# Folding the pooling map into w_out, and channel statistics from pair sums, in an 8-core streaming encoder layer

## The chip, the cores and the metric

The kernel runs as one program on the 8 cores of a Trainium2 chip, in two dies of four cores. Each core has TensorE (PE; its weight loads are shown apart as PEld), VectorE (DVE), ScalarE (ACT), GpSimd (POOL) and SyncE (SP), and 16 DMA engines. Every core computes its own stream with its own copy of the weights in its memory; the cores exchange nothing. The time is device time of the slowest core, in microseconds.

## The reference

One trunk layer, in float32. `x` is 8192 frames of a new stream (positions from 0) and 16 frames of a running one, of width 1024:

```python
z = x @ w_in + b_in                      # 1024 -> 1536: u (512) | a (512) | g (512)
v = a * sigmoid(g)
# mixer A: trailing mean over w frames (w = 2, 4, 8, 16, one group of 128 channels each) minus u
d = stack([(end - start) / count - u_new for each group])
A = einsum('blgc,gcd->blgd', d, w_pool) * pool_scale       # 4 maps of 128 x 128
# mixer B: causal depthwise convolution of width 31, LayerNorm over 512 channels, silu
B = silu(layer_norm(conv(v) + conv_b, ln_g, ln_b))
h = layer_norm(alpha * x + concat(A, B) @ w_out + b_out)
y = layer_norm(alpha * h + square(relu(h @ w_up)) @ w_down) # 1024 -> 4096 -> 1024
```

The outputs are `y`, and the last 15 rows of u and 30 of v of each stream. Beside the layer norms nothing is non-linear between `d` and `w_out`, which is what lets the pooling map and its scale be multiplied into the upper 512 rows of `w_out`.

## The kernel before

**Tiles.** A core's frames are cut into tiles of 512, the last 512 into two of 256; the 16 frames of the running stream ride with the second last tile. That makes 17 tiles, m = 0 to 16. Channels lie on the partitions for the input projection, the pooling, the convolution and the feed-forward up; frames lie on them for `w_out`, the down projection and both big layer norms.

**Weights.** They are 21 blocks of 1024 x 512 in f32 in `wblk`: b = 0 to 2 `w_in`, 3 and 4 `w_out`, 5 to 12 `w_up`, 13 to 20 `w_down`. A block comes into one of the four slots of the ring `wring` either by a casting DMA from `wblk`, issued by POOL, or by a plain DMA from `wscr`, a bf16 copy in memory, issued by SP. `LATE` names, for some blocks, the tile in which the copy is first stored; until then the block is cast anew each time. Blocks in `DIRECT` are cast from memory to memory, `wblk` to `wscr`. The three other first blocks lie in `rb` in tile 0. `paced` lets a first-round cast wait until the one two or three places before it has landed; POOL issues and waits in order, and SP too.

**PE's program** (`pe_thread`). It is: `inproj` of tile 0, `inproj(0)` of tile 1, `stats` (the channel sums of tile 0: eight matmuls against a matrix of ones), `poolmap` (four matmuls), `wout` of tile 0, the rest of tile 1's `inproj` with tile 0's `transposes`. From then on a round has `up` and `down` of tile m-1, with `poolmap` and `stats` of tile m inside the second half of `down`, then `inproj(0)` of tile m+1, `wout` of tile m, and so on. The round is the steady state. In every engine the order is fixed when the program is built: `Sched.run` takes the operation that can start first by estimated durations, with a small window in which the lower `prio` wins.

**The work off PE.** POOL makes the windows: `window` writes `dbf`, from which `poolmap` and, on ACT, `poolout` (L857) make the first four chunks of `mix`. DVE makes the convolution, 31 taps for each of four chunks of channels (L763; L714 in tile 0), into `acc`. Tile 0 is special: its chunks 0, 2 and 3 are on DVE (`conv0_dve`), chunk 1 is scaled by ACT (L729) and added up by POOL (L734, `conv0_pool`). `prep` then has ACT write `acc` and its square as bf16 (L796, L797); `stats` adds them up, `lnconv` and `lnapply` (L823 to L842) normalise and write the last four chunks of `mix`. `wout` needs all eight. POOL adds `b_out` to the rows of x (`xload`, L864), and the layer norms' gain and shift rows (L910, L912, L1022, L1024).

**Constant rows.** Five rows of 1024 (`rows`) are read by a broadcasting DMA to all 128 partitions (`late_loads`, L395, on ACT's queue, once tile 0's u is out), and three are scaled by ACT (L402).

## Time and profile before

| | before |
|---|---|
| time of the two runs shown, us | 2548.84 and 2615.7, median 2582.27 |
| the profiled execution, us | 2545.76 |
| its span on the slowest core (core 0), us | 2544.7 |
| spans of the other cores, us | 2533.2 to 2544.0 |
| mean granted TensorE clock, of full speed | 0.982 to 0.985 |
| busy, share of the span: PE, DVE, ACT, POOL | 95%, 74%, 47%, 51% |
| chain that ended last: on PE, on DMA, on DVE | 90%, 4%, 3% |
| PE busy in the 40 slices of 64 us | 4, 2, 9, 8, then 9 or more throughout |
| HBM read and written, MB | 486.68 and 55.82 |

The span runs from the first to the last instruction; 1.06 us of the profiled time lie outside it. The two runs shown differ by 2.6%; the lower one is near the profiled execution.

PE is busy in nearly all of the span, except for the first 130 us or so, and a little up to 260 us. A busy digit for PE says that matmuls were in flight, not how much they did.

### The profile page before, as it was taken

How to read it: one execution, taken by the hardware profiler on the slowest of the kernel's cores; microseconds unless marked ns; L12 is line 12 of the kernel's file. 1: busy time of each engine (PE TensorE's matmuls, PEld its weight loads, DVE VectorE, ACT ScalarE, POOL GpSimd, SP SyncE). 2: the span in 40 equal slices, each digit the busy share in tenths (PEclk: the TensorE clock that was granted, in tenths of full speed). 3: DMA queues.
4: the chain of work that ended last, by engine and by line, in shares of the span. 5: the costliest groups of instructions: out<-in, count | busy, mean ns of one | idle time of the engine just before them, and what ended most of it. 6: DMA issues, size and time to landing. Idle time of an engine off the chain costs nothing.

```text
span 2544.7 us, 39217 instructions; the slowest of 8 cores (2533.2 to 2544.7 us)
## 1 busy us (share of the span) xinstructions
...
## 2 busy tenths in 40 slices
...
GB/s 172 133 137 207 234 199 216 224 199 161 189 211 176 198 180 202 159 186 179 182 199 182 199 158 185 188 182 195 181 203 146 185 188 181 189 200 178 228 250 234
DMA packets 79184, 483.17 MB, mean 190 GB/s; under 512 B 11808, under 2 KB 12064, under 8 KB 29760
## 3 DMA queue, kind: packets, MB, share of 16 engines
...
q14 instruction: 108, 0.88, 0.1%
HBM read 486.68 MB, written 55.82 MB: 213 GB/s over the span
## 4 chain that ended last, share of the span: by engine, by line
PE 90%; DMA 4%; DVE 3%; issue 2%; ACT 0%; another core or an unknown queue 0%; POOL 0%; DVEq 0%; ACTq 0%; POOLq 0%; SPq 0%
PE bank L486 88%; DMA sb_wring<-wblk 2%; DVE bank L714 1%; DMA sb_wring<-wscr 1%; PE bank L940 1%; DMA sb_rb<-wblk 1%; PE bank L809 1%; PE bank L806 0%; DVE sb_acc L839 0%; DVE sb_stat L1004 0%; DVE sb_xr L1002 0%; DVE sb_xr L1044 0%; DVE sb_xr L1047 0%; ACT sb_rb L899 0%
## 5 line engine op out<-in xcount | busy, mean ns | idle before, releaser
L763 DVE SCALAR_TENSOR_TENSOR bank<-sb_vext,sb_params,bank 128x512 f32<-128x512 f32 (+1 forms) x1856 | 1169.5, 714 | 0.1
L486 PE MATMUL bank<-sb_wring,sb_rb 128*128 128x512 bf16 x4092 | 904.8, 380 | 6.8 <-DMA sb_wring<-wscr 3.1
L486 PE MATMUL bank<-sb_hT,sb_wring 128*128 128x512 bf16 (+2 forms) x4231 | 883.7, 368 | 22.2 <-DMA sb_wring<-wblk 15.4
L486 PEld LDWEIGHTS bank<-sb_hT,sb_wring 128*128 128x128 bf16 x4320 | 423.4, 98 | 479.7 <-issue 27.1
L486 PEld LDWEIGHTS bank<-sb_wring,sb_rb 128*128 128x128 bf16 (+1 forms) x4160 | 405.8, 98 | 497.2 <-issue 11.6
L977 ACT ACTIVATE sb_rtmp<-bank 128x512 f32<-128x512 f32 (+2 forms) x544 | 308.7, 571 | 185.0 <-PE bank L486 180.9
L978 ACT ACTIVATE sb_rb<-sb_rtmp 128x512 bf16<-128x512 f32 (+2 forms) x544 | 323.4, 604 | 41.2 <-ACT sb_rtmp L977 2.6
L922 POOL TENSOR_TENSOR sb_stat<-sb_stat,sb_cst 128x1 f32<-128x1 f32 x128 | 71.2, 556 | 519.1 <-DVE sb_stat L920 518.8
L486 PE MATMUL bank<-sb_xT,sb_wring 128*128 128x512 bf16 (+2 forms) x1477 | 314.0, 366 | 1.4
L1002 DVE TENSOR_TENSOR sb_xr<-bank,sb_xr 128x512 f32<-128x512 f32 x130 | 89.5, 688 | 284.7 <-PE bank L486 284.7
L864 POOL TENSOR_TENSOR sb_xr<-sb_xr,sb_row 128x1024 f32<-128x1024 f32 (+1 forms) x65 | 152.4, 2370 | 246.2 <-DMA sb_xr<-xp 246.1
L857 ACT ACTIVATE sb_mix<-bank,sb_params 128x512 bf16<-128x512 f32 (+2 forms) x68 | 39.8, 662 | 419.5 <-PE bank L486 419.5
L486 PE MATMUL bank<-sb_wring,sb_mix 128*128 128x512 bf16 (+1 forms) x1021 | 228.7, 381 | 7.5 <-ACT sb_mix L857 6.1
L486 PEld LDWEIGHTS bank<-sb_xT,sb_wring 128*128 128x128 bf16 x1504 | 144.9, 98 | 148.7 <-issue 0.4
L899 ACT ACTIVATE sb_rb<-sb_xr,sb_stat 128x1024 bf16<-128x1024 f32 (+1 forms) x65 | 80.5, 1238 | 203.0 <-POOL sb_stat L924 189.4
L486 PEld LDWEIGHTS bank<-sb_wring,sb_mix 128*128 128x128 bf16 (+1 forms) x1040 | 101.5, 98 | 132.0 <-issue 12.5
L1022 POOL TENSOR_TENSOR sb_xr<-sb_xr,sb_row 128x1024 f32<-128x1024 f32 (+1 forms) x63 | 148.2, 2364 | 14.8 <-ACT sb_xr L1020 14.8
L910 POOL TENSOR_TENSOR sb_xr<-sb_xr,sb_row 128x1024 f32<-128x1024 f32 (+1 forms) x65 | 152.1, 2362 | 0.2
L912 POOL TENSOR_TENSOR sb_xr<-sb_xr,sb_row 128x1024 f32<-128x1024 f32 (+1 forms) x65 | 152.0, 2358 | 0.3
L1024 POOL TENSOR_TENSOR sb_xr<-sb_xr,sb_row 128x1024 f32<-128x1024 f32 (+1 forms) x63 | 148.1, 2362 | 0.3
L824 DVE SCALAR_TENSOR_TENSOR sb_lnq<-bank,sb_lnq 128x512 f32<-128x512 f32 (+2 forms) x17 | 11.2, 660 | 177.7 <-ACT sb_lnq L823 177.7
L645 POOL TENSOR_TENSOR sb_ptmp<-sb_uext 128x526 f32<-128x526 f32 (+1 forms) x68 | 68.2, 1013 | 91.3 <-ACT sb_uext L623 91.3
...
## 6 DMA issues: line engine op xcount, KB each, us to landing
sb_wring<-wscr SPq DMA_DIRECT2D x323, 1024.0 KB, 5.2
...
sb_wring<-wblk POOLq DMA_DIRECT2D x27, 1024.0 KB, 13.2
sb_xT<-xpt POOLq DMA_DIRECT2D x14, 1024.0 KB, 10.6
wscr<-sb_wring SPq DMA_DIRECT2D x12, 1024.0 KB, 8.9
wscr<-wblk POOLq DMA_DIRECT2D x6, 1024.0 KB, 27.1
wscr<-sb_rb SPq DMA_DIRECT2D x3, 1024.0 KB, 14.7
```

Source lines behind the costliest of these rows:

```text
L486: ins = q.eng.matmul(o, l(), r(), start=first and i == 0, stop=last and i == len(items) - 1)
L763: yield Op(dve, tap(Tp), lambda e: e.scalar_tensor_tensor(out=o.ap[:, 0:Tp], in0=src.ap[:, k:k + Tp], scalar=wk, in1=p.ap[:, 0:Tp], op0=AL ...
L864: yield Op(pool, ptt(D), lambda e: e.tensor_tensor(out=x1.ap[0:n, :], in0=x0.ap[0:n, :], in1=rows[4][0:n, :], op=ALU.add), [x0, cv["row4"] ...
L899: yield Op(act, ac(D, 2), lambda e: e.activation(out=dst[0:n, :], in_=x.ap[0:n, :], func=AF.Identity, bias=s5.ap[0:n, 16:17], scale=s5.ap[ ...
L910: yield Op(pool, ptt(D), lambda e: e.tensor_tensor(out=x5.ap[0:n, :], in0=x4.ap[0:n, :], in1=rows[0][0:n, :], op=ALU.mult), [x4, cv["row0" ...
L912: yield Op(pool, ptt(D), lambda e: e.tensor_tensor(out=x6.ap[0:n, :], in0=x5.ap[0:n, :], in1=rows[1][0:n, :], op=ALU.add), [x5, cv["row1"] ...
L922: yield Op(pool, 0.6, lambda e: e.tensor_tensor(out=s4.ap[0:n, 15:16], in0=s3.ap[0:n, 14:15], in1=cst[0:n, 0:1], op=ALU.pow), [s3, cv["mha ...
L977: yield Op(act, ac(n), lambda e: e.activation(out=t.ap[:, 0:n], in_=o.ap[:, 0:n], func=AF.Relu), [o], [t], 3)
L978: yield Op(act, ac(n), lambda e: e.activation(out=r.ap[:, 0:n], in_=t.ap[:, 0:n], func=AF.Square), [t], [r], 3)
L1002: yield Op(dve, dv(512), lambda e: e.tensor_tensor(out=x2.ap[0:n, sl], in0=o.ap[0:n, :], in1=x.ap[0:n, sl], op=ALU.add), [x, o], [x2], 2)
L1022: yield Op(pool, ptt(D), lambda e: e.tensor_tensor(out=x4.ap[0:n, :], in0=x3.ap[0:n, :], in1=rows[2][0:n, :], op=ALU.mult), [x3, cv["row2" ...
L1024: yield Op(pool, ptt(D), lambda e: e.tensor_tensor(out=x5.ap[0:n, :], in0=x4.ap[0:n, :], in1=rows[3][0:n, :], op=ALU.add), [x4, cv["row3"] ...
```

## The change

**The pooling map.** `poolmap` and `poolout` are gone. The windows write the first four chunks of `mix` themselves. Before tile 0's `wout`, `w_pool` is loaded transposed, scaled by `pool_scale` (four ACT instructions), and multiplied in f32 on PE with the upper 512 rows of `w_out` (`fold`: eight matmuls; the rows come by four plain f32 DMAs into `xr`, `fold_loads`, released by the first matmuls of tile 0's `inproj(2)`); ACT casts the results into the two ring slots of blocks 3 and 4 (`fold_out`, eight instructions). The casting DMAs of these two blocks bring only the lower half. Both blocks must now be stored from tile 0, so `LATE` has new entries: 3 and 4 leave it, 7 comes in.

**The statistics.** `prep` waits for two chunks. Then one engine adds the pair of chunks (`pairsum`), ACT squares each into f32 and the same engine adds the squares (`pairsq`). That engine is DVE for tiles 0 to 3 and POOL from tile 4. `stats` is four matmuls, not eight.

**The constant rows** come as one partition each, at the start; PE spreads them by ten f32 matmuls against a row of ones, between tile 0's `inproj(1)` and `inproj(2)`, and ACT writes them out.

**Four casts.** The first four blocks of `DIRECT`, once spawned after `stats`, stand behind block 7 in the list of first casts, each paced like the others. Tile 0's rows of x are asked for before `inproj(2)`.

```diff
-LATE = {1: 1, 3: 2, 4: 1, 2: 2, 6: 1, 9: 2, 12: 3, 15: 1, 18: 3}
+LATE = {1: 1, 6: 1, 15: 1, 2: 2, 9: 2, 18: 2, 7: 3, 12: 3}
...
-                yield Op(act, 0.1, lambda e: e.dma_start(out=rows[i][:], in_=rows_in[i:i + 1, :].broadcast_to([128, D])), [],
-                         [cv[f"raw{i}"]], 2, sem="load", mb=0.53)
+                yield Op(act, 0.1, lambda e: e.dma_start(out=rows[i][0:1, :], in_=rows_in[i:i + 1, :]), [], [cv[f"raw{i}"]], 2,
+                         sem="load", mb=0.01)
...
+        def spread():
+            for i in (4, 0, 1, 2, 3):
+                banks_ = [Val(R, 1), Val(R, 1)]
+                for h in range(2):
+                    o = banks_[h]
+                    items = [(lambda: ones_f[0:1, :], lambda: rows[i][0:1, h * 512:(h + 1) * 512], [cv["onesf"], cv[f"raw{i}"]])]
+                    yield group(lambda: o.ap[:], o, items, 0.9)
+                S.spawn(spread_out(i, banks_))
...
+                if kind == "direct":
+                    r = paced(wsv[b])
+                    yield Op(pool, 0.6, lambda e: e.dma_start(out=wscr[b], in_=wblk[b]), r, [wsv[b]], prio=0, sem=dsem(), mb=2.1)
+                    continue
...
+                elif key in ((0, 3), (0, 4)):
+                    w = wo_v[b - 3][0]
+                    r = paced(w)
+                    yield Op(pool, 0.6, lambda e: e.dma_start(out=w.ap[:, 2048:4096], in_=wblk[b][:, 2048:4096]), r, [w],
+                             prio=0, sem="load2", mb=1.05)
...
+        def fold():
+            for h in range(2):
+                for g in range(4):
+                    o = Val(R, 1)
+                    items = [(lambda: wpf[:, g * 128:(g + 1) * 128], lambda: wo_f[g].ap[:, h * 512:(h + 1) * 512], [wps[4], wo_f[g]])]
+                    yield group(lambda: o.ap[:], o, items, 0.9)
+                    S.spawn(fold_out(h, g, o))
+
+        def fold_out(h, g, o):
+            a, b = wo_v[h][g], wo_v[h][g + 1]
+            yield Op(act, ac(512), lambda e: e.copy(out=b.ap[:, g * 512:(g + 1) * 512], in_=o.ap[:]), [o, a], [b], 3)
...
-                self.d = [Val(DB[c], 1) for c in range(4)]
+                self.d = self.mix[0:4]
...
-                yield Op(act, ac(T), lambda e: e.copy(out=cb.ap[:, 0:T], in_=a.ap[:, 0:T]), [a], [cb], 2)
-                yield Op(act, ac(T), lambda e: e.activation(out=qb.ap[:, 0:T], in_=a.ap[:, 0:T], func=AF.Square), [a], [qb], 2)
+            def pairsum(self, p):
+                T = self.T
+                a, b, cb = self.acc[2 * p], self.acc[2 * p + 1], self.cb[p]
+                q, d = (dve, dv(T)) if self.m < 4 else (pool, 0.23 + 0.00203 * T)
+                yield Op(q, d, lambda e: e.tensor_tensor(out=cb.ap[:, 0:T], in0=a.ap[:, 0:T], in1=b.ap[:, 0:T], op=ALU.add),
+                         [a, b], [cb], 2)
...
+                if i == 0 and b == 7:
+                    for d in DIRECT[0:4]:
+                        order.append((None, d, 0, "direct"))
...
-            for b in range(3):
-                yield from t0.inproj(b, ("f", b))
+            yield from t0.inproj(0, ("f", 0))
+            yield from t0.inproj(1, ("f", 1))
+            yield from spread()
+            for c in range(t0.nch):
+                S.spawn(t0.xload(c))
+            yield from t0.inproj(2, ("f", 2))
...
-                                if h == 1 and qd == 0:
-                                    yield from nx.poolmap()
...
                 if i == 0:
-                    for c in range(t0.nch):
-                        S.spawn(t0.xload(c))
+                    yield from fold()
                     yield from t0.stats()
-                    S.spawn(direct(DIRECT[0:4]))
-                    yield from t0.poolmap()
```

In the orders below L761 is the new line of L714 and L756 that of L709, L781 of L734, L853 is `pairsum`, L864 of the new program is `pairsq` (in the old program L864 is the sum of x and `b_out`, now L917), L454 is a cast of memory to memory, L471 the same before.

**DVE at the end of tile 0's convolution, before:** chunk 0 is done, then twelve taps end chunk 2, then chunk 3 runs alone to its end.

```order
24 L714 SCALAR_TENSOR_TENSOR sb_acc<-sb_vext,sb_params,bank 128x512
25 L714 SCALAR_TENSOR_TENSOR bank<-sb_vext,sb_params,bank 128x512 x12
26 L714 SCALAR_TENSOR_TENSOR sb_acc<-sb_vext,sb_params,bank 128x512
27 L709 TENSOR_SCALAR bank<-sb_vext,sb_params 128x512
28 L714 SCALAR_TENSOR_TENSOR bank<-sb_vext,sb_params,bank 128x512 x29
29 L714 SCALAR_TENSOR_TENSOR sb_acc<-sb_vext,sb_params,bank 128x512
```

And in the changed kernel:

```order
27 L761 SCALAR_TENSOR_TENSOR sb_acc<-sb_vext,sb_params,bank 128x512
28 L756 TENSOR_SCALAR bank<-sb_vext,sb_params 128x512
29 L761 SCALAR_TENSOR_TENSOR bank<-sb_vext,sb_params,bank 128x512
30 L853 TENSOR_TENSOR sb_btmp<-sb_acc 128x512
31 L864 TENSOR_TENSOR sb_btmp<-sb_sqf 128x512
32 L761 SCALAR_TENSOR_TENSOR bank<-sb_vext,sb_params,bank 128x512 x28
33 L761 SCALAR_TENSOR_TENSOR sb_acc<-sb_vext,sb_params,bank 128x512
34 L853 TENSOR_TENSOR sb_btmp<-sb_acc 128x512
35 L864 TENSOR_TENSOR sb_btmp<-sb_sqf 128x512
```

The sums of the first pair (chunks 0 and 1) stand in the middle of chunk 3's taps, two rows after it has begun. Chunk 1 comes from POOL.

**POOL in tile 0, before:** the last chunk-1 adds stand among the windows, and the four casts stand behind the windows and behind the sums of x.

```order
38 L734 TENSOR_TENSOR sb_acc<-sb_acc,sb_rtmp 128x512
39 L656 TENSOR_SCALAR sb_ptmp<-sb_ptmp 128x512
...
59 L660 TENSOR_TENSOR sb_dbf<-sb_ptmp,sb_uext 128x512
60 L665 TENSOR_TENSOR sb_dbf<-sb_stat,sb_uext 128x15
61 L864 TENSOR_TENSOR sb_xr<-sb_xr,sb_row 128x1024 x4
62 L471 DMA wscr<-wblk 32x16384 x4
63 L457 DMA sb_wring<-wblk 128x4096
```

And in the changed kernel:

```order
31 L454 DMA wscr<-wblk 32x16384
32 L781 TENSOR_TENSOR sb_acc<-sb_acc,sb_lnq 128x512
33 L781 TENSOR_TENSOR sb_acc<-sb_acc,sb_lnA 128x512
34 L781 TENSOR_TENSOR sb_acc<-sb_acc,sb_rtmp 128x512 x2
35 L781 TENSOR_TENSOR sb_acc<-sb_acc,sb_lnq 128x512
36 L781 TENSOR_TENSOR sb_acc<-sb_acc,sb_lnA 128x512
37 L692 TENSOR_TENSOR sb_ptmp<-sb_uext 128x526 x2
...
40 L703 TENSOR_SCALAR sb_ptmp<-sb_ptmp 128x512
41 L454 DMA wscr<-wblk 32x16384
42 L707 TENSOR_TENSOR sb_mix<-sb_ptmp,sb_uext 128x512
```

The first cast now stands before the last six adds of chunk 1, the second and third inside the windows, the fourth behind them; all of chunk 1 is ahead of the windows.

**POOL in a steady round, before (tile 5):**

```order
305 L912 TENSOR_TENSOR sb_xr<-sb_xr,sb_row 128x1024 x2
306 L907 TENSOR_SCALAR sb_xr<-sb_xr,sb_stat 128x1024 x2
307 L910 TENSOR_TENSOR sb_xr<-sb_xr,sb_row 128x1024 x2
308 L912 TENSOR_TENSOR sb_xr<-sb_xr,sb_row 128x1024 x2
309 L570 DMA sb_xT<-xpt 128x4096
310 L864 TENSOR_TENSOR sb_xr<-sb_xr,sb_row 128x1024 x4
```

And in the changed kernel (same tile):

```order
327 L965 TENSOR_TENSOR sb_xr<-sb_xr,sb_row 128x1024
328 L616 DMA sb_xT<-xpt 128x4096
329 L853 TENSOR_TENSOR sb_btmp<-sb_acc 128x512
330 L864 TENSOR_TENSOR sb_btmp<-sb_sqf 128x512
331 L917 TENSOR_TENSOR sb_xr<-sb_xr,sb_row 128x1024 x4
```

The sums of the second pair stand ahead of the four sums of x; those of the first pair stand earlier, among the rows L960 to L965 (old L907 to L912).

## Rows read from the trace of the kernel before

**Rows 1.** Waits of PE over the whole span: for whom, us, times, longest.

```profile
PE bank L806 <- DVE sb_acc L714: 45.7, 1, 45.7
...
PE bank L486 <- DMA sb_wring<-wblk: 15.4, 4, 9.1
...
PE bank L486 <- DMA sb_wring<-wscr: 4.0, 3, 2.5
```

**Rows 2.** Stretches: length, busy us of each engine, then granted clock, DMA share, GB/s.

```profile
640.00:2400.00 1760.00, 1748.08 (x8384) 819.93 (x8545) 1345.70 (x2260) 850.33 (x1327) 899.37 (x723) 1.00 0.55 185
```

**Rows 3.** One stretch in tile 0's round, columns as before.

```profile
96.00:120.00 24.00, 6.83 (x15) 1.78 (x15) 18.98 (x20) 11.22 (x17) 23.12 (x24) 0.50 0.11 44
```

**Rows 4.** Timeline, a steady round: start, us, engine, line, [idle before].

```profile
1149.62 1.03 PE L486 MATMUL bank<-sb_dbf,sb_wpool_bf 128*128 128x512 bf16 x4
1149.66 9.29 POOL L864 TENSOR_TENSOR sb_xr<-sb_xr,sb_row 128x1024 f32<-128x1024 f32 x4 [17.64 <-DMA sb_xr<-xp]
...
1150.48 13.98 PE L486 MATMUL bank<-sb_wring,sb_rb 128*128 128x512 bf16 x63
...
1154.69 1.40 DVE L763 SCALAR_TENSOR_TENSOR sb_acc<-sb_vext,sb_params,bank 128x512 f32<-128x512 f32 x2
1155.52 0.62 ACT L796 CAST sb_btmp<-sb_acc 128x512 bf16<-128x512 f32 x1 [3.00 <-DVE sb_acc L763]
...
1164.51 0.81 PE L806 MATMUL bank<-sb_btmp,sb_ones_bf 128*128 128x512 bf16 x3
...
1166.02 7.29 PE L486 MATMUL bank<-sb_wring,sb_rb 128*128 128x512 bf16 x33
...
1170.60 2.50 DVE L839 TENSOR_TENSOR sb_acc<-sb_acc,sb_lnA 128x512 f32<-128x512 f32 x4 [0.53 <-ACT sb_lnA L830]
```

**Rows 5.** Timeline of PE, 0 to 290 us.

```profile
48.12 7.07 PE L486 MATMUL bank<-sb_xT,sb_rb 128*128 128x512 bf16 x31 [1.65 <-DMA sb_xT<-xpt]
...
187.61 8.75 PE L486 MATMUL bank<-sb_hT,sb_wring 128*128 128x512 bf16 x32 [2.13 <-DMA sb_wring<-wblk]
205.44 15.29 PE L486 MATMUL bank<-sb_hT,sb_wring 128*128 128x512 bf16 x62 [9.07 <-DMA sb_wring<-wblk]
```

**Rows 6.** Timeline of POOL, 0 to 170 us.

```profile
40.30 1.28 POOL L734 TENSOR_TENSOR sb_acc<-sb_acc,sb_rtmp 128x512 f32<-128x512 f32 x1
...
53.57 1.28 POOL L734 TENSOR_TENSOR sb_acc<-sb_acc,sb_lnq 128x512 f32<-128x512 f32 x1 [4.63 <-ACT sb_lnq L729]
...
85.65 1.26 POOL L734 TENSOR_TENSOR sb_acc<-sb_acc,sb_lnA 128x512 f32<-128x512 f32 x1 [8.94 <-ACT sb_lnA L729]
...
92.98 1.26 POOL L734 TENSOR_TENSOR sb_acc<-sb_acc,sb_rtmp 128x512 f32<-128x512 f32 x1 [0.20 <-POOL sb_acc L734]
...
122.62 2.07 POOL L471 DMA_DIRECT2D wscr<-wblk  x4
```

**Rows 7.** Timeline of DVE, 0 to 170 us.

```profile
75.03 24.81 DVE L714 SCALAR_TENSOR_TENSOR bank<-sb_vext,sb_params,bank 128x512 f32<-128x512 f32 x29
99.95 0.75 DVE L714 SCALAR_TENSOR_TENSOR sb_acc<-sb_vext,sb_params,bank 128x512 f32<-128x512 f32 x1
```

**Rows 8.** Timeline of all engines, 98 to 123 us.

```profile
104.36 1.91 PE L809 MATMUL bank<-sb_btmp,sb_ones_bf 128*128 128x512 bf16 x4
...
111.33 6.83 DVE L839 TENSOR_TENSOR sb_acc<-sb_acc,sb_lnA 128x512 f32<-128x512 f32 x4 [0.53 <-ACT sb_lnA L830]
...
112.08 10.59 POOL L864 TENSOR_TENSOR sb_xr<-sb_xr,sb_row 128x1024 f32<-128x1024 f32 x4
...
119.78 3.23 PE L486 MATMUL bank<-sb_wring,sb_mix 128*128 128x512 bf16 x7 [6.08 <-ACT sb_mix L857]
```

**Rows 9.** DMA issues by line, 96 to 270 us: count, size, median us to landing.

```profile
wscr<-wblk POOLq DMA_DIRECT2D x6, 1024.0 KB, 27.1
wscr<-sb_wring SPq DMA_DIRECT2D x3, 1024.0 KB, 15.3
```

**Rows 10.** Timeline of PE, 1000 to 1180 us: `stats` one round earlier.

```profile
1015.10 0.81 PE L806 MATMUL bank<-sb_btmp,sb_ones_bf 128*128 128x512 bf16 x3
```

124 lines of the change are left out of this document (77 added, 47 removed).

## The prediction

> **What bounds the kernel now.** I read the stretches first. From 640 to 2400 us PE is busy 1748 of 1760 us at a granted clock of 1.00, DVE 1346, POOL 899, and the DMA engines work at 0.55 of their time [rows 2]. So over most of the span a matmul taken out is time won, as long as nothing PE waits for comes later than now. The waits of PE say where it is not the bound: one of 45.7 us for the convolution of tile 0 on DVE, then 15.4 and 4.0 us for weight blocks [rows 1]. The timelines say when. PE has nothing from the end of tile 1's first block (48.12 + 7.07) to about 100.8 [rows 5]; `wout` gets going at 119.78 [rows 8]; and from there to about 255 us it stands four or five times for weight DMAs, the longest 9.07 us at 205.44 [rows 5]. Of the 15.4 us, 3.8 belong to the first blocks near 30 us, and of the 4.0, 0.8 to the last rounds, so 11.6 + 3.2 = 14.8 us fall between 170 and 255. In front of them the DMA engines are nearly idle: share 0.11 from 96 to 120 us [rows 3], until POOL issues the four memory-to-memory casts in one go at 122.62 [rows 6]. The kernel is thus a steady part bound by PE, behind a start bound first by DVE and then by the weight DMAs.
>
> **Steady rounds.** Between 1150.48 and 1166.02 PE ran 64 matmuls of `down` and the 8 of `stats` in 15.54 us, 0.216 us each [rows 4] (records of one or two are missing, the starts count). The pooling map's four start at 1149.62 and the next group at 1150.48: 0.86 us, the same price. A round loses four matmuls of the map and four of `stats`: 8 x 0.216 = 1.73 us. Tiles 1 to 14 give 14 x 1.73 = 24.2. Tile 15 has 272 columns and gives 0.9; tile 16, where PE already waits for DVE at `stats`, I put at 0. Together **-25.1 us**.
>
> TensorE's granted clock is 1.00 here, its upper level of 2.4 GHz [rows 2]. The Trainium skill, TensorE: Matmul & The Clock Gate (HAM trace caveats under Seeing it yourself), says to budget 1.95 GHz for dense matmuls on all cores. By that the 25.1 would be some 31 us; the row decides, and this trace does not agree with the page.
>
> What must be on time for this? In the round shown the last `acc` is ready at 1154.69 + 1.40 = 1156.1 and `stats` began near 1164.5 [rows 4]; without the map it begins 0.86 earlier, at 1163.6, so the cover is 7.5 us. In it now lie a sum on POOL, two squares on ACT beside it and a second sum on POOL. Nearest rows: a POOL sum of two 128x512 f32 tiles 1.26 to 1.28 us [rows 6], an ACT pass of that size 0.62 [rows 4]. That is 0.1 + 1.3 + 1.3, about 2.7 us, and leaves 4.8. The sums of x, 9.29 us on POOL, used to start at 1149.66 [rows 4]; they now queue behind, run from 1159 to 1168, and are wanted by `wout`, which comes 96 matmuls behind `stats`, at about 1186. POOL sat idle 17.64 us before them, which hides the first pair's two sums and what they wait for ACT. In tiles 1 to 3 DVE does the sums, 4 x 0.63 us by the undisturbed L839 (2.50 for four) [rows 4] and 4 x 1.7 by the disturbed one (6.83 for four) [rows 8]: 2.5 to 6.8 us against 7.5. I take 0.
>
> **Start, the convolution chain.** This is where the change can lose. DVE ran chunk 3 alone at 24.81 / 29 = 0.856 us a tap, from 74.2 to 100.7 [rows 7]. Now the sums of pair 0 stand two rows into it, at about 75.9, and need chunk 1 from POOL. POOL finished chunk 1 only at 92.98 + 1.26 = 94.2 [rows 6], with two long stalls on the way, 4.63 and 8.94 us, both while ACT issued or awaited the broadcast rows, and three windows in between. Those go away. From the add at 40.30 there were 25 to do at 1.47 us (1.27 and a gap of 0.20): 36.9, and four DMA issues of 0.52 in between add 1.4, which gives **78.6** at best. ACT also feeds the chain, and between its scalings it now has ten row copies and the outputs of `inproj(2)` and of tile 1's first block, which come later by the spread; I add 3 to 4 and take 82. DVE then stands from 75.9 to 82.1, makes a sum, waits for the square of chunk 1, makes the other (1.5 together), and has 29 taps at 0.856 = 24.8 left: chunk 3 ends at 108.4, against 100.7 now. That is +7.7 us.
>
> Behind it things get shorter. The last matmul of `stats` ended near 106.3 [rows 8], 5.6 after DVE's last tap, part of it because ACT's copy of the pooling history stood in front of the casts. Now it is one sum beside two squares, another sum and two matmuls at the low clock (0.43 us each), 2.6: 111.0, so +4.7. Next the map's outputs no longer stand last before `wout` (6.08 us of wait for L857 [rows 8]). The four L839 took 6.83 us beside POOL's sums of x (112.08 to 122.67) [rows 8], against 2.50 alone [rows 4]; POOL is through its windows some 10 us earlier, so they meet only in part: -1 to -4. PE can also do the first seven products of `wout` before the last chunk arrives: -1. I carry **+1 us**, with -4 (chunk 1 at 78.6) and +8 (at 90) as ends.
>
> The GPSIMD Engine Reference of the Trainium skill (Specifications) says that GpSimd shares its SBUF interfaces with VectorE and that they contend when a DVE instruction has two SBUF inputs. The new pair sums are of that kind, which speaks against the change; the trace agrees, by the 6.83 and 2.50 above.
>
> **The ten spread and eight fold matmuls** are in f32, which no row shows. Lower bound: as bf16, 18 x 0.216 = 4 us. Upper: each operand is twice as wide, so I reckon four passes at the low clock of 0.5 [rows 3] with 0.43 us each, 1.7 us, 31 us in all. I take four passes at the full clock for the spread, 8.6 us, and at the low one for the fold, 13.7. They lie in PE's gap of 45.7 us, so they cost nothing up to about 2.5 us each; beyond, they delay `stats`. The spread's other effect, on ACT, is in the 82. The eight casts of the fold (0.6 us each) run on ACT while chunk 3 is computed.
>
> **The weight DMAs.** The four casts took a median of 27.1 us to land [rows 9], and the ring blocks issued behind them waited in the same queue. They are now issued at about 73, 84, 91 and 103 (POOL's new order, with the durations above), and run in the time that was empty: with the 24 us of little DMA work [rows 3] filled and the broadcast rows gone (5 x 128 x 4 KB, 2.6 MB), the queue is some 30 us ahead. The ring blocks that PE waited for were late by at most 9.07. The stalls of 14.8 us go, and with them the low clock behind three of them: 8.75 us for 32 matmuls and 15.29 for 62 [rows 5] against 6.9 and 13.4 at 0.216, and a third like these, some 5 us. The ends are 0 and 19.8. Against the full gain: blocks 3 and 4 are now stored in tile 0, two of 15.3 us [rows 9] on SP, ahead of the other stores that free ring slots. I take **-17**.
>
> **Sum.** -25.1 + 1 - 17 = -41.1. From the profiled execution, 2545.76, that gives **2505 us**. The runs shown are 2548.84 and 2615.7; I take the profiled one and the lower run as the kernel's time, not their median of 2582.
>
> **Rivals.**
> - *The DMA stalls stay in part.* A slot is reloaded only when its store is done, and SP issues stores in order; two more are ahead. For it speaks that a cast and a store of a block take about as long as PE needs for four blocks. Against it, the queue is 30 us ahead. With 10 of the 20 us kept: 2515.
> - *Chunk 1 is late.* The casts on POOL wait for the landing of the one three before. If that, or ACT held by a slow spread, puts chunk 1 at 90, the chain ends 8 us later: 2512.
> - *Statistics late in the steady rounds.* If POOL's second pair comes 7 us later than reckoned, PE waits 2 us in each of 12 rounds (tiles 4 to 15): 2529.
> - *Slower than before.* The same mechanism, at `stats`. Beyond its cover of 4.8 us each microsecond costs 12. It makes up for the 41 us at 3.4 us beyond, so if the second pair is over 8.2 us late, as it would be were POOL's four sums of x (9.29 us) in front of it: 12 x 4.5 = 54 us, 2559. The order has them behind.
> - *All falls well.* Chunk 1 at 78.6 and no DMA stall left: 25.1 + 4 + 19.8 = 49, 2497; it passes 2% only with a gain in the last tiles too.
>
> **How the numbers follow.** My forecast (2499 to 2511) 0.50; DMA stalls stay 0.17; chunk 1 late 0.12; statistics late, 2517 to 2540, 0.10; slower 0.03; all well, to 2492, 0.08. The range of 2491 to 2533 leaves out the slower case, most of the upper half of the late statistics, and little below. Two per cent, about what a measurement of this kernel can tell from no change, is 51 us: only the far end of "all well" and an underrated DMA gain pass 2495, 0.10; slower by over 2% needs statistics 12.5 us late, 0.02; within 2%, 0.88.
>
> **What would show it.** Right: rounds of 147.7 us instead of the 1164.51 - 1015.10 = 149.4 [rows 4, 10], no wait of PE at `stats` from tile 1 on, DMA share near 1 from 96 to 120, no weight stall above 2 us between 130 and 255, chunk 3 ending near 108, `wout` going near 120. Wrong: a wait of DVE at the first pair's sum of over 10 us, a PE wait at L874 in each round, POOL idle before L454 on a DMA, or SP still storing when a slot is wanted.

## The result, and the profile after

| | before | changed |
|---|---|---|
| runs, us | 2548.84 and 2615.7 | 2517.43 and 2517.59 |
| the profiled execution, span of core 0, us | 2544.7 | 2516.4 |
| spans of the eight cores, mean, us | 2540.6 | 2511.7 |

The ratio is 0.9887, with a 95% interval of 0.987 to 0.9903: a little over 1% faster, within the 2% band. Forecast were 2505, and 2491 to 2533 as a range. The range held the time; the forecast gain of 41.1 us came to 28.3 on core 0 and 28.9 as a mean of the cores. (One die sometimes runs slowly whatever the kernel, as in the 2615.7; below, only executions without that are compared.)

The whole argument fits into three stretches, each read off the timelines of PE: to the start of tile 0's `w_out` (the row that waits for the last chunk of `mix`), from there to the start of tile 1's `stats`, and from there to the end.

| change in us | forecast | core 0 | mean of 8 cores |
|---|---|---|---|
| to `w_out` of tile 0 | +1 | +9.5 | +7.9 |
| `w_out` to `stats` of tile 1 | -17.9 | -17.9 | -15.3 |
| `stats` of tile 1 to the end | -24.2 | -19.9 | -21.6 |

(The forecast's 25.1 for the steady part stands here as 24.2 in the third row and 0.9, tile 1's map, in the second.)

The waits of PE over the whole span, changed kernel, core 0; they answer to [rows 1]:

```profile
PE bank L874 <- DVE sb_acc L761: 24.6, 1, 24.6
PE bank L531 <- DMA sb_rb<-wblk: 16.9, 1, 16.9
PE bank L531 <- DMA sb_xr<-wblk: 9.6, 2, 6.8
PE bank L531 <- ACT sb_mix L910: 5.7, 1, 5.7
PE bank L531 <- DMA sb_wring<-wblk: 5.3, 2, 4.0
...
PE bank L874 <- DVE sb_btmp L853: 4.1, 1, 4.1
PE bank L874 <- DVE sb_acc L810: 1.8, 1, 1.8
```

Of the weight waits of the old kernel one is left behind the start, 1.2 us. The wait for the convolution is shorter only because the new f32 work stands in the same gap, as the timeline of PE shows (start, us, [idle before]; it answers to [rows 5]):

```profile
29.46 8.75 PE L531 MATMUL bank<-sb_hT,sb_wring 128*128 128x512 bf16 x32 [4.04 <-DMA sb_wring<-wblk]
38.15 15.24 PE L531 MATMUL bank<-sb_row,sb_ones_f 1*128 1x512 f32 x20
53.32 9.10 PE L531 MATMUL bank<-sb_hT,sb_wring 128*128 128x512 bf16 x32
62.26 7.07 PE L531 MATMUL bank<-sb_xT,sb_rb 128*128 128x512 bf16 x32
76.17 2.05 PE L531 MATMUL bank<-sb_xr,sb_wpf 128*128 128x512 f32 x2 [6.83 <-DMA sb_xr<-wblk]
...
115.77 0.58 PE L874 MATMUL bank<-sb_btmp,sb_ones_bf 128*128 128x512 bf16 x1 [24.60 <-DVE sb_acc L761]
120.45 0.59 PE L874 MATMUL bank<-sb_btmp,sb_ones_bf 128*128 128x512 bf16 x1 [4.11 <-DVE sb_btmp L853]
```

`w_out` starts at 129.32, against 119.78 [rows 8]. On all eight cores it starts 41.4 to 41.5 us after POOL's last add of chunk 1, so the start hangs on that chunk. It did before too: there `w_out` starts 25.5 us after the last add of chunk 1 on seven of the eight cores, while the end of chunk 3 on DVE moves by 3 us from core to core without moving it. So already before, `w_out` followed POOL's work on chunk 1 and what stands behind it; the prediction reckons the start from DVE's convolution alone.

On DVE (answering to [rows 7]):

```profile
75.99 0.76 DVE L761 SCALAR_TENSOR_TENSOR bank<-sb_vext,sb_params,bank 128x512 f32<-128x512 f32 x1
87.98 1.47 DVE L853 TENSOR_TENSOR sb_btmp<-sb_acc 128x512 bf16<-128x512 f32 x1 [11.23 <-POOL sb_acc L781]
89.37 1.54 DVE L864 TENSOR_TENSOR sb_btmp<-sb_sqf 128x512 bf16<-128x512 f32 x1
90.83 23.93 DVE L761 SCALAR_TENSOR_TENSOR bank<-sb_vext,sb_params,bank 128x512 f32<-128x512 f32 x28
114.87 0.75 DVE L761 SCALAR_TENSOR_TENSOR sb_acc<-sb_vext,sb_params,bank 128x512 f32<-128x512 f32 x1
115.72 4.58 DVE L853 TENSOR_TENSOR sb_btmp<-sb_acc 128x512 bf16<-128x512 f32 x1
...
126.30 2.50 DVE L907 TENSOR_TENSOR sb_acc<-sb_acc,sb_lnA 128x512 f32<-128x512 f32 x4 [0.53 <-ACT sb_lnA L898]
```

On POOL (answering to [rows 6]), with two of its stalls for ACT, the first of the four casts, the last add of chunk 1, and the sums of x:

```profile
52.11 1.26 POOL L781 TENSOR_TENSOR sb_acc<-sb_acc,sb_lnA 128x512 f32<-128x512 f32 x1 [5.56 <-ACT sb_lnA L776]
...
55.54 1.25 POOL L781 TENSOR_TENSOR sb_acc<-sb_acc,sb_rtmp 128x512 f32<-128x512 f32 x1 [1.65 <-ACT sb_rtmp L776]
...
78.70 0.54 POOL L454 DMA_DIRECT2D wscr<-wblk  x1
...
86.61 1.26 POOL L781 TENSOR_TENSOR sb_acc<-sb_acc,sb_lnA 128x512 f32<-128x512 f32 x1 [0.20 <-POOL sb_acc L781]
...
110.52 9.24 POOL L917 TENSOR_TENSOR sb_xr<-sb_xr,sb_row 128x1024 f32<-128x1024 f32 x4
```

And on ACT, the copies of the spread rows that stand between chunk 1's scalings:

```profile
46.66 1.28 ACT L413 ACTIVATE sb_row<-bank 128x512 f32<-128x512 f32 x2 [1.52 <-PE bank L531]
50.07 1.29 ACT L413 ACTIVATE sb_row<-bank 128x512 f32<-128x512 f32 x2 [2.13 <-PE bank L531]
51.26 0.71 ACT L776 ACTIVATE sb_lnA<-sb_vext,sb_params 128x512 f32<-128x512 f32 x1
```

So the first pair's sum stopped DVE for 11.2 us, and the second pair's sum took 4.58 us where 0.69 is its price with POOL quiet (below), beside the sums of x.

A steady round, from the timelines of PE, DVE, ACT and POOL (answering to [rows 4, 10]):

```profile
998.09 0.60 PE L874 MATMUL bank<-sb_btmp,sb_ones_bf 128*128 128x512 bf16 x2
...
1137.41 1.40 DVE L810 SCALAR_TENSOR_TENSOR sb_acc<-sb_vext,sb_params,bank 128x512 f32<-128x512 f32 x2
1138.30 1.23 ACT L861 ACTIVATE sb_sqf<-sb_acc 128x512 f32<-128x512 f32 x2 [32.38 <-DVE sb_acc L810]
1138.97 1.26 POOL L853 TENSOR_TENSOR sb_btmp<-sb_acc 128x512 bf16<-128x512 f32 x1 [24.60 <-ACT sb_sqf L861]
1140.19 1.25 POOL L864 TENSOR_TENSOR sb_btmp<-sb_sqf 128x512 bf16<-128x512 f32 x1
1141.41 9.29 POOL L917 TENSOR_TENSOR sb_xr<-sb_xr,sb_row 128x1024 f32<-128x1024 f32 x4
...
1145.78 0.60 PE L874 MATMUL bank<-sb_btmp,sb_ones_bf 128*128 128x512 bf16 x2
```

The round is 1145.78 - 998.09 = 147.69 us, 1.73 below the old 149.42 (the mean of thirteen rounds), which is what was forecast, and the sums are done 4.3 us before `stats`.

### The profile page after: what moved, and what is told of

It is laid out like the page before. It is cut to its first block, busy times and chain, and to the rows that moved or that the text cites. A ratio compares the mean times of both kernels' runs of the same rounds, so it can differ in the third digit from the quotient of the medians.

```text
span 2516.4 us, 39111 instructions; the slowest of 8 cores (2506.9 to 2516.4 us)
## 1 busy us (share of the span) xinstructions
PE 2429.7 (97%) x11808; PEld 1139.3 (45%) x11808; DVE 1918.4 (76%) x3187; ACT 1150.0 (46%) x1800; POOL 1364.5 (54%) x1116
## 4 chain that ended last, share of the span: by engine, by line
PE 94%; DVE 2%; DMA 2%; POOL 1%; issue 1%; ACT 0%; DVEq 0%; POOLq 0%; ACTq 0%
PE bank L531 92%; DMA sb_wring<-wblk 1%; PE bank L993 1%; DVE bank L761 1%; POOL sb_acc L781 1%; DMA sb_rb<-wblk 1%; PE bank L877 0%; PE bank L874 0%; DVE sb_stat L946 0%; DVE sb_xr L942 0%; DVE sb_btmp L853 0%; DVE sb_stat L1057 0%; DVE sb_xr L1055 0%; DVE sb_xr L1097 0%; DVE sb_xr L1100 0%
## 5 line engine op out<-in xcount | busy, mean ns | idle before, releaser
L531 PE MATMUL bank<-sb_wring,sb_rb 128*128 128x512 bf16 (+1 forms) x4160 | 906.4, 380 | 1.2 <-DMA sb_wring<-wblk 1.2
L531 PE MATMUL bank<-sb_xT,sb_wring 128*128 128x512 bf16 (+2 forms) x1504 | 319.6, 368 | 0.0
L861 ACT ACTIVATE sb_sqf<-sb_acc 128x512 f32<-128x512 f32 (+2 forms) x68 | 38.8, 601 | 491.2 <-DVE sb_acc L810 473.5
L917 POOL TENSOR_TENSOR sb_xr<-sb_xr,sb_row 128x1024 f32<-128x1024 f32 (+1 forms) x65 | 152.6, 2372 | 76.0 <-DMA sb_xr<-xp 75.9
L853 POOL TENSOR_TENSOR sb_btmp<-sb_acc 128x512 bf16<-128x512 f32 (+2 forms) x26 | 30.9, 1188 | 279.4 <-ACT sb_sqf L861 267.3
L531 PEld LDWEIGHTS bank<-sb_wring,sb_mix 128*128 128x128 bf16 (+1 forms) x1040 | 101.9, 98 | 133.3 <-issue 13.9
L965 POOL TENSOR_TENSOR sb_xr<-sb_xr,sb_row 128x1024 f32<-128x1024 f32 (+1 forms) x65 | 153.3, 2364 | 1.9
L892 DVE SCALAR_TENSOR_TENSOR sb_lnq<-bank,sb_lnq 128x512 f32<-128x512 f32 (+2 forms) x17 | 11.2, 661 | 135.7 <-ACT sb_lnq L891 135.7
```

The source lines that it names most:

```text
L531: ins = q.eng.matmul(o, l(), r(), start=first and i == 0, stop=last and i == len(items) - 1)
L917: yield Op(pool, ptt(D), lambda e: e.tensor_tensor(out=x1.ap[0:n, :], in0=x0.ap[0:n, :], in1=rows[4][0:n, :], op=ALU.add), [x0, cv["row4"] ...
L965: yield Op(pool, ptt(D), lambda e: e.tensor_tensor(out=x6.ap[0:n, :], in0=x5.ap[0:n, :], in1=rows[1][0:n, :], op=ALU.add), [x5, cv["row1"] ...
```

## The experiments

Fourteen runs. All positions below are means over the eight cores of the profiled execution, since one core's start varies by some 5 us (core 0 of the changed kernel started `w_out` at 129.3 once and at 124.9 another time); "times" are those of the slowest core. The runs were made in five series on several chips, the kernel before beside each of them, at 2545.5 to 2559.6, and once at 2568.8. There is one trace of each kernel: the changed one, traced twice, had mean spans of 2511.7 and 2515.4 (2513.8 without its one late core), so that a difference of 2 or 3 us in that column alone shows little. "Cast lead" is how long before `w_out`'s start POOL issued the first of the four casts; "waits" are PE's waits for weight blocks between `w_out`'s start and 300 us, per core.

| kernel | `w_out` starts | to tile 1's `stats` | waits | cast lead | mean span | times |
|---|---|---|---|---|---|---|
| before | 118.4 | 145.6 | 12.6 | -2.2 | 2540.6 | 2548.8 |
| changed | 126.3 | 130.3 | 1.3 | 50.6 | 2511.7 | 2517.4-2517.6 |
| c_changed | 129.8 | 130.0 | 1.1 | 52.9 | 2515.4 | 2519.5, 2527.3 |
| e1_casts_alone | 125.1 | 131.7 | 1.9 | 31.0 | 2535.0 | 2537.9, 2538.2 |
| e2_pairs_02_13 | 129.2 | 130.2 | 1.6 | 52.4 | 2515.1 | 2522.5-2529.2 |
| e3_spread_late | 123.7 | 131.5 | 2.4 | 43.2 | 2509.4 | 2513.2-2515.3 |
| e4_both | 120.7 | 131.9 | 2.5 | 39.5 | 2507.4 | 2510.5-2512.8 |
| e6_xsums_behind | 122.9 | 130.7 | 1.8 | 46.7 | 2508.0 | 2513.5-2515.2 |
| e7_tile0_eight | 125.8 | 128.7 | 0.7 | 48.9 | 2509.0 | 2514.3-2524.3 |
| e8_best | 119.8 | 130.9 | 1.5 | 39.5 | 2505.9 | 2508.0-2531.4 |
| e5_casts_back | 124.4 | 133.1 | 3.8 | 9.6 | 2511.7 | 2517.5-2527.9 |
| e9_best_loads | 114.3 | 131.8 | 1.7 | 31.6 | 2500.1 | 2505.3-2505.9 |
| e10_rows_alone | 118.6 | 140.7 | 8.8 | 3.8 | 2536.4 | 2540.6-2544.6 |
| e11_rows_back | 120.1 | 134.3 | 4.3 | 11.6 | 2508.7 | 2513.8-2518.8 |
| e12_table_alone | 124.0 | 149.1 | 15.7 | -2.8 | 2550.1 | 2553.7, 2555.0 |
| e13_best_casts_back | 114.2 | 133.0 | 3.2 | 14.4 | 2502.0 | 2505.8, 2507.2 |

### The casts alone, in the old kernel

```diff
+                if i == 0 and b == 7:
+                    for d in DIRECT[0:4]:
+                        order.append((None, d, 0, "direct"))
...
-                    S.spawn(direct(DIRECT[0:4]))
```

> The kernel before with one part of the change alone: the first four casts of memory to memory stand behind block 7 and are paced. Theory 1 (the weight term of the prediction was right, 17 us): the waits for weight blocks between 170 and 255 us, 14.8 us in the kernel before, fall below 3 us, and the time is that of the profiled execution before less 15 to 19 us, 2527 to 2531. Rival (the waits went in the changed kernel only because its w_out starts 9.5 us later there and leaves the transfers that time): here w_out goes at about 120 as before, half or more of the waits stay, and the time is 2535 to 2541.

The waits fell from 12.6 to 1.9 us a core and the second stretch by 13.9 us, though `w_out` started only 6.7 later. But the end gained just 5.6 on average and the time was 2538, which lies in the rival's range but not by its mechanism. In this kernel POOL issues casts inside the windows and between its sums of x, and DVE's multiplications by `lnA` meet those sums for longer: 11.69 us for the four, 7.54 of it one of them, against 6.83 in [rows 8]. Half of what the weights give is lost in the head. A step moved ahead of others on an in-order engine has its price there.

### The first pair without POOL's chunk

In tile 0 the pairs are (0,2) and (1,3), so that DVE need not wait for chunk 1 in the middle of chunk 3.

```diff
-                if self.ready[c // 2] == 2:
+                p = c % 2 if self.m == 0 else c // 2
+                self.ready[p] += 1
+                if self.ready[p] == 2:
```

> The changed kernel, in tile 0 with the pairs (0,2) and (1,3) instead of (0,1) and (2,3), so that DVE's first pair sum needs no chunk from POOL. Theory 1 (the convolution chain lost its time at DVE's wait of 11.2 us for POOL's chunk 1, and the end gets it back): that wait is gone, chunk 3 ends at about 103, w_out gets going 8 to 12 us before the 129.3 of the changed kernel, and the time is 2506 to 2510. Rival A (weights absorb it: an earlier w_out stands again for the weight transfers): the start is as early, but waits for weight blocks grow between 170 and 255 us, and the time is 2514 to 2518. Rival B (the contention with POOL takes it back at the normalisation): w_out goes at 124 to 129.

On core 0, DVE and POOL (L855 and L866 are the two pair sums, L919 the sums of x):

```profile
79.80 1.53 DVE L866 TENSOR_TENSOR sb_btmp<-sb_sqf 128x512 bf16<-128x512 f32 x1 [4.65 <-ACT sb_sqf L863]
...
105.69 9.23 POOL L919 TENSOR_TENSOR sb_xr<-sb_xr,sb_row 128x1024 f32<-128x1024 f32 x4
107.07 0.75 DVE L761 SCALAR_TENSOR_TENSOR sb_acc<-sb_vext,sb_params,bank 128x512 f32<-128x512 f32 x1
107.92 7.56 DVE L855 TENSOR_TENSOR sb_btmp<-sb_acc 128x512 bf16<-128x512 f32 x1
```

Each theory got a piece. The wait for POOL is gone, but DVE stands 4.65 us for a square instead: ACT, in its fixed order, makes it behind chunk 1's scalings, and those wait for POOL. Chunk 3 so ends at 107.8, not 103, and its sum then stands until POOL has finished all four sums of x (rival B). `w_out` went at 124.5 on this core, 4.8 earlier, but most of that is this core's chunk 1, which came 4.0 earlier than in the trace of the changed kernel. Counted from the end of chunk 1, `w_out` goes 40.6 us later instead of 41.4, so the new pairs gained 0.8; the theory's 8 to 12 was far off, because the first pair's square stands behind chunk 1's scalings on ACT, and the second pair's sum behind POOL's sums of x, which follow chunk 1. Beyond that, one core (3) went at 143.9, because one of the fold's loads landed some 30 us late. Nobody had foreseen that; it set the 2529.2 of the traced execution.

### The spread in PE's gap, alone and with the pairs

```diff
-            yield from spread()
...
                 if i == 0:
+                    yield from spread()
                     yield from fold()
```

> The changed kernel with the ten f32 matmuls of the spread moved behind the first block of tile 1, into the gap of PE. Theory 1 (the spread, 15.2 us on PE with ACT standing behind it, is what made chunk 1 late): chunk 1 ends on POOL at 80 to 84 instead of 87.9, DVE waits 4 to 7 us instead of 11.2, and the time is 4 to 8 us below the changed kernel's 2517.5. Rival (POOL's own work sets chunk 1, since window steps now slip in among its sums): chunk 1 ends at 86 to 88 and the time stays within 2 us of 2517.5.

> Both edits together: the pairs (0,2) and (1,3) in tile 0, and the spread behind the first block of tile 1. If DVE's wait for chunk 1 was the whole loss, the second edit adds nothing to the first: within 1.5 us of the kernel with the pairs alone. If an earlier end of POOL's windows and of its sums of x takes contention away from the normalisation, 2 to 4 us more, 2503 to 2507.

With the spread moved, chunk 1 ended at 82.4 (mean) instead of 84.9, `w_out` 2.6 earlier, the time at 2513 to 2515, about half of the 4 to 8 us of the theory. Steps of the windows now slip in among chunk 1's adds, and the stretched sum has only moved: on core 0 DVE still waited 8.39 us for POOL, and the first pair's sum then took 5.37 us beside POOL's window steps, where it took 1.47 in the changed kernel, while the second pair's took 0.69 instead of 4.58. From chunk 1's end to `w_out` are 41.0 us, much as before. Both edits gave 5.6 us at `w_out` (37.6 from the end of chunk 1) and 4.3 in the mean span; the second edit did add to the first, so that DVE's wait was not the whole loss. The time, 2510.5 to 2512.8, is above the 2503 to 2507 expected.

### The changed kernel again, and three repairs

`e6` holds POOL's sums of x in tile 0 back until the first normalised chunk of `mix` is there; `e7` has the old eight-matmul statistics in tile 0 only; `e8` puts the repairs together, with four buffers for squares and the first pair's sum of squares behind chunk 3.

```diff
+                late = [self.mix[4]] if self.m == 0 else []
+                for v in late:
+                    v.left += 1
...
-                         [x0, cv["row4"]], [x1], 7)
+                         [x0, cv["row4"]] + late, [x1], 7)
```

> The changed kernel itself once more, beside the three others of this series, to see how far its landmarks move from run to run: w_out of tile 0 going at 126.3 us as a mean over the cores (124.2 to 130.2), tile 1's stats at 257.1 (252.9 to 261.3), time 2515 to 2520.

> The changed kernel, with POOL's four sums of x in tile 0 held back until the first of the normalised chunks of mix is written, so that none runs beside DVE's second pair sum. Theory 1 (DVE's sum of two chunks in SBUF stands still while POOL goes through its sums of x, which made it 4.6 us long in the changed kernel and up to 7.6 in the one with the pairs (0,2) and (1,3)): DVE's second pair sum takes 0.7 to 1.0 us, the four multiplications by lnA 2.5 as now, w_out goes 3.5 to 4 us earlier, 122 to 123 as a mean, and the time is 2 to 4 us below the changed kernel. Rival (it only reads long because it waits for a square or for chunk 3): the 4.6 us stay. Second rival: the sums of x are now late for the rows of w_out, and what DVE gains it waits for there.

> The changed kernel with the eight-matmul statistics of before in tile 0 only (ACT writes each chunk and its square as bf16, DVE makes no pair sum there). Theory 1 (the pair sums cost the head 11.2 us of wait, 3.0 us of DVE work and the 4.6 us sum, and the end gets most of it back): chunk 3 ends at 101 to 102, w_out goes at 117 to 121 as a mean over the cores unless the multiplications by lnA meet the sums of x (then up to 125), and the time is 3 to 7 us below the changed kernel. Rival (the weight transfers absorb an earlier w_out): w_out is earlier by as much, but tile 1's stats stay at 256 to 257 and the time within 1 us of the changed kernel.

> All the repairs of tile 0 together: pairs (0,2) and (1,3), the spread behind tile 1's first block, the sums of x behind the normalisation, four buffers for squares, and the first pair's sum of squares behind chunk 3. Theory 1: DVE runs chunk 3 without a stop from about 74, it ends at 100.5 to 102, w_out goes at 110 to 113 as a mean, 8 to 10 us before the kernel with both edits (120.7). If two thirds of an earlier w_out reach the end, as they did from the changed kernel to the one with both edits (5.6 at w_out, 4.0 at tile 1's stats), the time is 2504 to 2508. Rival (the weights of tile 1's round cannot come sooner): waits for weight blocks of 5 us and more return between 170 and 255 us and the time stays at 2510 to 2513.

The repeat shows how far the changed kernel itself moves: its times are 2519.5 and 2527.3, the latter outside the 2515 to 2520 expected, and in the profile of that one it is one core's fold load again, for which PE waits 29.5 us (core 1):

```profile
124.76 7.58 PE L531 MATMUL bank<-sb_xr,sb_wpf 128*128 128x512 f32 x10 [29.48 <-DMA sb_xr<-wblk]
...
143.02 7.33 PE L531 MATMUL bank<-sb_wring,sb_mix 128*128 128x512 bf16 x20 [6.55 <-ACT sb_mix L910]
```

`e6` answers for the 4.58 us cleanly. DVE, then POOL, core 0:

```profile
116.19 0.69 DVE L853 TENSOR_TENSOR sb_btmp<-sb_acc 128x512 bf16<-128x512 f32 x1
...
125.90 9.29 POOL L920 TENSOR_TENSOR sb_xr<-sb_xr,sb_row 128x1024 f32<-128x1024 f32 x4 [15.35 <-ACT sb_mix L910]
```

The sum takes 0.69 on every core, `w_out` goes 3.4 us earlier (3.8 counted from the end of chunk 1, on every core) and the mean span falls by 3.7. In `e7` chunk 3 ends at 101.0 and, on the six cores without a late load, `w_out` starts at 121.6 (their multiplications by `lnA` meet the sums of x: 7.9 us for four on core 1, 11.4 on the other five) and the span is 2505.2, 6.5 us below the changed kernel's first trace and 8.6 below the second without its late core. The pair sums in tile 0 so cost some 6 to 9 us net, while they pay 0.86 in each later tile. The time, 2514.3 to 2524.3, shows none of it, since two cores of the traced execution had late loads. `e8` started `w_out` at 111.8 to 115.2 on five cores, whose spans are 2495.8 to 2503.4, and at 126 to 137 on three whose fold loads were late. Its times are 2508 to 2531, not the 2504 to 2508 expected. An earlier start is not absorbed by the weights: on the five cores the second stretch took 131.4 us, against 130.3.

### The late loads, and the casts put back

`e5` is the changed kernel with the four casts behind `stats` again; `e9` is `e8` with one guard:

```diff
-                    r = paced(wsv[b])
+                    r = paced(wsv[b]) + (wo_f if b == DIRECT[0] else [])
```

> The changed kernel with the four casts of memory to memory back where they were, spawned behind tile 0's stats. Theory 1 (the weight term, 16 to 17 us, and the starved fold loads both come from the casts' new place): waits for weight blocks of 8 to 15 us a core return between 170 and 265 us, tile 1's stats move from about 257 to 266 to 272, the time is 2528 to 2536; and no fold load lands after 105 us on any core, where in four of the seven profiled kernels with both the fold and the early casts some core had one at 114 to 133. Rival for the loads (their lateness has to do with the three casts into rb before them): late loads are there as often as before. Rival for the time (an w_out that starts 8 us later than in the old kernel already hides the transfers): below 2522.

> The kernel with all the repairs of tile 0, and besides the first of the four casts waits until the fold's four loads have landed. Theory 1 (what made that kernel 2508 to 2531 from run to run is a fold load that shares the DMA engines with these casts and lands up to 35 us late on one core or three; its cores without that took 2496 to 2503): no load lands after 95 us, w_out goes at 111 to 116 on every core, all spans lie within 2494 to 2506, and the time is 2502 to 2507 in every run. Rival (the loads are late for another reason): the outliers at 2510 to 2531 stay. Second rival (POOL, waiting for the loads, is late with its windows or the casts are late for tile 0's feed-forward): w_out at 116 to 120, or waits for weights of over 4 us, 2508 to 2513.

With the guard no load was late on any core, `w_out` went at 113.3 to 115.7, and four executions lie within 0.6 us, at 2505.3 to 2505.9: 0.9828 (0.9791 to 0.9866) of the kernel before. POOL's wait and the start of `w_out`, slowest core (4):

```profile
83.81 0.58 POOL L454 DMA_DIRECT2D wscr<-wblk  x1 [2.73 <-DMA sb_xr<-wblk]
...
115.12 15.73 PE L531 MATMUL bank<-sb_wring,sb_mix 128*128 128x512 bf16 x60 [5.72 <-ACT sb_mix L912]
```

Counted over all profiled kernels with a fold: where the casts are early and unguarded, on 8 of 64 cores the fold ended after 105 us (114 to 133); where they are guarded or back behind `stats`, on none of 32. In each of the eight cases one load took 62 to 74 us to land. That speaks for the casts as the cause; it isn't settled, since one execution of `e5`, without a trace, had two cores at 2523 and 2527, with a mean granted clock of 0.978 where its others had 0.983 to 0.985.

`e5` was the surprise. I expected 8 to 15 us of weight waits to return; 3.8 did, and the mean span is that of the changed kernel. So the term "weights" had the right size for a reason that was not, or not alone, the one given.

### What relieves the weights

Three more parts, each tried alone: the constant rows as one partition and a spread, in the old kernel (`e10`); the casts and the broadcast rows both back, in the changed one (`e11`); the new `LATE` table in the old kernel (`e12`); and all repairs with the casts back (`e13`).

```diff
-LATE = {1: 1, 3: 2, 4: 1, 2: 2, 6: 1, 9: 2, 12: 3, 15: 1, 18: 3}
+LATE = {1: 1, 6: 1, 15: 1, 2: 2, 9: 2, 18: 2, 7: 3, 12: 3}
```

> The kernel before with another part of the change alone: the constant rows come as one partition each and PE spreads them (as in the changed kernel), the four casts stay behind stats. The question is where the 13 us of waits for weight blocks go when the casts are NOT moved: the changed kernel with its casts put back still had only 3.8 us a core (133.1 us from w_out's start to tile 1's stats, against 145.6 in the kernel before). Theory 1 (the broadcast rows, 2.6 MB in front of the first casts, held the weight queue): here w_out to stats takes 131 to 137 us, waits fall to 2 to 6 us a core, and the time is 2536 to 2543 unless the spread delays w_out itself. Rival (the later w_out and the halved casts of blocks 3 and 4 made the room, the rows did not): w_out to stats stays at 142 to 146 us and the time at 2545 to 2552.

> The complement: the changed kernel with the casts back behind stats and the constant rows back on broadcasting transfers. Theory 1 (the rows held the queue): w_out to tile 1's stats returns to 140 to 146 us, with 8 to 13 us of waits for weight blocks a core, where the same kernel without the broadcast rows had 133.1 and 3.8. Rival (the rows matter little): 131 to 136 us. In the head the spread's 15.2 us on PE are gone, but ACT issues and awaits five broadcasts again, so that POOL's chunk 1 ends at 88 to 95 instead of 84.8.

> The kernel before with one more part of the change alone: the new LATE table, so that blocks 3 and 4 are stored from tile 0 and tile 1 loads them instead of casting them anew (7 is cast once more instead). Casts, rows, statistics and map as before. Theory 1 (with neither the moved casts nor the point-wise rows the changed kernel still had only 4.3 us of waits, so the table is what relieves the weights): w_out to tile 1's stats falls from 145.6 us to 133 to 138, and the time is 2535 to 2541. Rival (the halved casts of blocks 3 and 4, with the fold, or w_out's other start did it): 143 to 147 us, 2546 to 2552.

> The kernel with all the repairs of tile 0 and the four casts back behind stats (so no guard is needed). Theory 1 (the moved casts and the table are substitutes wherever w_out starts): w_out at 112 to 115, from there to tile 1's stats 133 to 136 us against 131.9 with the casts moved and guarded, and the time is 2505 to 2511, with no outlier core. Rival (the 8 us later w_out of the changed kernel is what hid the transfers when the casts were put back): 139 to 145 us, 8 us and more of waits, 2512 to 2520.

My theories on `e10`, `e11` and `e12` all fell: the rows alone took away 4 us of waits of 12.6, putting them back cost 0.5, and the table alone made it worse (15.7 us; and its `w_out`, again 25.5 us behind chunk 1 on every core, starts 5.6 us later with it, for a reason that was not followed up). In `e11` chunk 1 was also not late, 88 to 95 as I expected, but the earliest of all, 80.3: ACT waits for the broadcast rows there behind almost all of chunk 1's scalings. So the stalls of chunk 1 in the kernel before came from where ACT's order put these waits, more than from the broadcasts as such. `e12`, PE of core 0:

```profile
212.78 4.42 PE L486 MATMUL bank<-sb_hT,sb_wring 128*128 128x512 bf16 x10 [10.64 <-DMA sb_wring<-wblk]
```

These kernels line up by the cast lead. Lead and waits, in us: -2.8 and 15.7, -2.2 and 12.6, 3.8 and 8.8, 9.6 and 3.8, 11.6 and 4.3, 14.4 and 3.2, 31.0 and 1.9, 50.6 and 1.3. POOL issued the four casts at 122.6 in the old kernel [rows 6]; in the changed one with the casts "back", at 111.67 on core 0, since POOL's chunk 1 and windows are done sooner, while `w_out` starts later:

```profile
111.67 2.08 POOL L516 DMA_DIRECT2D wscr<-wblk  x4
```

In this series ten microseconds of lead go with nearly all of the gain; the other forty that the change buys bring 2.5 us of waits, and the late fold loads. No run moved the lead alone between 4 and 10 us. The three kernels with 9.6 to 14.4 also have the fold, and so only half of blocks 3 and 4 to cast; `e1`, at 31.0, has not, and shows that lead suffices in the old kernel. What the halved casts do by themselves is open. `e13` shows that a later `w_out` is not needed: with 114.2 the second stretch is 133.0 us, and its times, 2505.8 and 2507.2 (0.9826, 0.9802 to 0.9849), are those of `e9` within the interval. Between the two I see no measured difference; `e9`'s mean span is 2.0 us lower, no more than one trace differs from the next.

## Why the prediction was right or wrong, point by point

The forecast on core 0 missed by 12.8 us: 8.5 in the start's convolution chain, 4.3 in the last tiles, nothing in sum in the stretch with the weights and in the steady rounds. That the time still fell inside the range is the width of the range. Of the signs named for being wrong the first one came: DVE waited 11.2 us at the first pair's sum.

**Steady rounds: right.** 8 x 0.216 = 1.73 us a round; thirteen rounds from `stats` of tile 1 (268.01, now 259.64) to that of tile 14 (2210.43, now 2179.61) gained 22.45 us. No wait of PE at `stats` in between; the cover of 4.8 us was 4.3. The rivals "statistics late" and "slower than before" did not happen.

**The last tiles: mis-sized, by 4.3 us on core 0 and 2.7 in the mean.** From `stats` of tile 14 on I reckoned -1.8 us; core 0 lost 2.5, the mean 0.9. On core 0 PE waits 4.3 instead of 3.2 us for the rows of tiles 14 and 15, and at `stats` of tile 16 it waits 2.7 us, 1.8 for DVE's last chunk and 0.9 for POOL's two sums, where the old kernel waited 1.45 at the map and `stats` together. The sums, hidden in a full round, are on the path there, and "I put at 0" had no row behind it. On cores 0 and 3 the granted clock was also low right behind the first of these waits (ten transposes in 1.22 us; 0.73 on the six others). Core 0, then core 5:

```profile
2218.18 1.22 PE L993 MATMUL bank<-sb_identb,sb_rb 128*128 128x128 bf16 x10 [1.89 <-ACT sb_rb L952]
...
2422.36 0.27 PE L874 MATMUL bank<-sb_btmp,sb_ones_bf 128*128 128x256 bf16 x1 [0.60 <-POOL sb_btmp L853]
```

```profile
2219.43 0.73 PE L993 MATMUL bank<-sb_identb,sb_rb 128*128 128x128 bf16 x10 [1.89 <-ACT sb_rb L952]
```

Why the wait itself grew in tile 15 (1.43 to 2.44 us) was not tested.

**The convolution chain: the step that failed.** "I carry **+1 us**" was +9.5 on core 0, beyond even my end of +8, and +7.9 in the mean of the cores. Two terms of it were too small, and both sit behind POOL, on which the start hangs. (a) "I add 3 to 4 and take 82" for chunk 1: it ended at 87.9 (84.9 in the mean), nearly the 90 of the rival, as ACT waited for PE's f32 results between its scalings. With the two sums at 2.85 us instead of 1.5, chunk 3 ended at 115.6, not 108.4: 7.2 us. (b) "one sum beside two squares, another sum" in 2.6 us to the end of `stats`: it took 6.1, 3.9 of it the stretched sum. I had reckoned the contention with POOL for the multiplications by `lnA` and credited the change with escaping it (they do take 2.50 now, and that stretch was 2.2 shorter than forecast), but not asked which DVE instruction stands beside the sums of x instead. `e6` prices (b) at 3.4 to 3.8 us, `e7` the pair sums of tile 0 at some 6 to 9 in all. In `e2` DVE's wait of 11.2 us was gone, but a wait of 4.65 for a square and 3.0 more of stretched sum came in its place, and the start gained 0.8.

**The f32 matmuls: hidden, but at the wrong clock.** They cost PE nothing directly, as forecast. Four passes were right, the full clock was not. The stretch of the spread:

```profile
38.00:53.40 15.40, 15.40 (x22) 5.70 (x22) 15.40 (x22) 7.90 (x13) 7.54 (x8) 0.58 1.00 201
```

At the granted 0.58, ten matmuls of four passes at 0.216 / 0.58 are 14.9 us; 15.24 was measured, against the 8.6 I took. The clock was at its upper level when the spread began, went to 0.50 during the third of its ten matmuls, and was back at 1.00 only 4 us behind the last, though PE was never idle in it. Until 38.15 PE had run matmuls over 128 rows; those of the spread have one. What this costs: `e5` and `e11` differ in the rows alone, and chunk 1 ends at 84.8 with the spread and at 80.3 without it, `w_out` starts at 124.4 and at 120.1, and the mean spans are 2511.7 and 2508.7. In the changed kernel with the casts back this part brought nothing and probably cost, though 3.0 us of mean span are at the edge of what one trace each can show; in the old one, `e10`, it gave 4.2 us in the mean span.

**The weight DMAs: size right, cause half right.** -17 forecast, -15.3 to -17.9 with the 0.9 of the map in it. The casts do it in the old kernel (`e1`), but in the changed kernel with the casts put back all but 2.8 us of it stayed (`e5`). POOL's earlier freedom is the likeliest reason, by the series of leads; the halved casts of blocks 3 and 4 were not tried apart. That POOL would be free "some 10 us earlier" stands in my own text, for another term; I did not ask what it does to the casts queued behind. The reservation about blocks 3 and 4 stored ahead did not come true in the changed kernel, where one wait of 1.2 us is left; in the old one the table alone added 3 us (`e12`). The 2.6 MB of broadcast rows counted for 4 us of waits in the old kernel and 0.5 in the changed one. As forecast, the DMA share from 96 to 120 us is 1 (1.08, where it was 0.11).

**Not foreseen:** the fold's loads, late by 20 to 35 us on a core now and then. One set the slowest core in the changed kernel's execution of 2527.3, and its time, between 2517 and 2527, needs more than two runs to be known.
